# Two modulated norms of a transformer pair by units of two k-tiles through four PSUM banks, evacuated by VectorE alone

## What is computed

```python
def rms_norm_2(x, g):
    y = x32 * lax.rsqrt(jnp.mean(x32 * x32, axis=-1, keepdims=True) + EPS)
    return (y * g).astype(x.dtype)

def modulate(h, shift, scale):
    return h * (1.0 + scale[:, None, :]) + shift[:, None, :]
```

## Time and profile before

| | us |
|---|---|
| median of 3 runs (2705.98 to 2708.37) | 2708.1 |
| profiled execution, its time | 2709.32 |
| its span | 2707.5 |
| TensorE busy | 2627.9 (97%) |
| VectorE busy | 1789.3 (66%) |
| ScalarE busy | 1229.5 (45%) |
| DMA: moved, rate over the span | 581 MB, 215 GB/s |
| granted TensorE clock, mean | 0.988 |

### The profile page before, as it was taken

One profiled execution on the slowest core, in us unless ns is written; L12 is line 12 of the kernel. 1 busy time (PEld: TensorE's weight loads), 2 busy tenths in 40 slices (PEclk: granted clock), 3 DMA queues, 4 the chain that ended last, 5 costly groups with the idle time before them and its releaser, 6 DMA issues.

```text
span 2707.5 us, 35204 instructions
## 1 busy us (share of the span) xinstructions
PE 2627.9 (97%) x12256; PEld 2191.1 (81%) x12256; DVE 1789.3 (66%) x2084; ACT 1229.5 (45%) x1468; POOL 16.0 (1%) x23
## 2 busy tenths in 40 slices
PE   7999999999999999999999899998799999999998
PEld 6888887888878888888888788887678888888886
DVE  5766656557677777777776667875665565555565
ACT  5444456454454444444444544455444443444343
POOL 0000000000000000000000000000000000000000
PEclk9999999999999999999999999999899999999999
DMA  7865555566887777777777577774547666766664
GB/s 269 267 206 167 167 158 184 168 215 195 263 276 250 251 249 249 251 250 249 250 250 243 168 218 216 212 221 132 194 156 223 207 213 200 223 213 207 212 213 133
DMA packets 305304, 581.36 MB, mean 215 GB/s; under 512 B 17728, under 2 KB 28112, under 8 KB 304672
## 3 DMA queue, kind: packets, MB, share of 16 engines
q1 hardware_dynamic: 303664, 573.60, 67.3%
q0 software_dynamic: 1520, 6.11, 0.8%
HBM read 577.53 MB, written 2.11 MB: 214 GB/s over the span
## 4 chain that ended last, share of the span: by engine, by line
PE 85%; DVE 6%; DMA 3%; ACT 3%; issue 2%; SPq 0%; DVEq 0%; ACTq 0%
PE acc L1124 79%; PE W L1124 4%; DVE wlo L1577 2%; DMA raw<-in_w_in 1%; ACT whi L538 1%; PE W L1184 1%; DVE adaacc L1599 1%; DMA raw<-in_w_ffn_in 1%; DMA raw<-in_w_out 1%; ACT arena L565 0%; ACT arena L760 0%; DVE arena L1887 0%; PE W L1296 0%; DVE arena L2185 0%; PE acc L1427 0%
## 5 line engine op out<-in xcount | busy, mean ns | idle before, releaser
L1577 DVE TENSOR_TENSOR wlo<-raw,whi 128x1024 fp32r<-128x1024 f32 x888 | 1080.8, 1224 | 765.2 <-ACT whi L538 762.0
L538 ACT ACTIVATE whi<-raw 128x1024 fp32r<-128x1024 f32 x888 | 934.7, 1059 | 1175.6 <-PE acc L1124 938.4
L1124 PE MATMUL acc<-whi,hH 128*128 128x512 f32 x2528 | 694.0, 396 | 25.7 <-ACT whi L538 19.0
L1124 PE MATMUL acc<-whi,hL 128*128 128x512 f32 x2528 | 679.7, 391 | 0.0
L1124 PE MATMUL acc<-wlo,hH 128*128 128x512 f32 x2528 | 678.4, 390 | 0.0
L1124 PEld LDWEIGHTS acc<-whi,hH 128*128 128x128 f32 x2528 | 470.5, 189 | 119.8 <-issue 27.8
L1124 PEld LDWEIGHTS acc<-whi,hL 128*128 128x128 f32 x2528 | 476.9, 189 | 101.4
L1124 PEld LDWEIGHTS acc<-wlo,hH 128*128 128x128 f32 x2528 | 476.1, 188 | 100.4
L1124 PE MATMUL acc<-whi,yH 128*128 128x512 f32 x992 | 271.0, 395 | 4.8 <-issue 4.8
L1599 DVE SCALAR_TENSOR_TENSOR adaacc<-raw,cs,adaacc 128x512 f32<-128x512 f32 x360 | 269.8, 749 | 8.6 <-DMA raw<-in_w_ada 1.7
L1124 PE MATMUL acc<-wlo,yH 128*128 128x512 f32 x992 | 266.3, 390 | 0.0
(11 more groups left out here) (190 smaller groups left out, 981.4 us busy)
## 6 DMA issues: line engine op xcount, KB each, us to landing
raw<-in_w_in SPq DMA_DIRECT2D x264, 512.0 KB, 4.4
raw<-in_w_ada SPq DMA_DIRECT2D x192, 512.0 KB, 4.7
raw<-in_w_ffn_in SPq DMA_DIRECT2D x176, 512.0 KB, 4.6
raw<-in_w_up SPq DMA_DIRECT2D x128, 512.0 KB, 4.6
raw<-in_w_down SPq DMA_DIRECT2D x128, 512.0 KB, 4.5
raw<-in_w_ffn_out SPq DMA_DIRECT2D x88, 512.0 KB, 4.9
raw<-in_w_out SPq DMA_DIRECT2D x32, 512.0 KB, 5.3
raw<-in_w_o SPq DMA_DIRECT2D x32, 512.0 KB, 4.5
```

Of the source, the lines that this page charges most:

```text
L538: act.activation(whi[:, v], raw[:, s], ACT.Copy).then_inc(S("w_hi"), 1)
L1124: return pe.matmul(o, l, r, start=start, stop=stop, skip_group_check=True)
L1577: dve.tensor_tensor(wlo[:, v], raw[:, s], whi[:, v].bitcast(F32), ALU.subtract)\
```

## The change

- **Units.** The norm goes by eight units of two k-tiles, as the weights do. `scale`, the transposes (4 each), the evacuation, `hH` and `hL` are all by unit, and each weight unit of the first group waits for its own `hL`.
- **Ring.** A unit's transposes go to one of four PSUM banks (`ring`): two of `W`, two of one half of `acc`. TensorE transposes units 0 to 3 ahead of weight unit 0, and unit `u + 4` as a hook behind weight unit `u`, once VectorE has evacuated unit `u` (`h_mod`).
- **Evacuation.** VectorE evacuates both tiles of a unit. ScalarE only copies to `hH`.
- **Column sums.** At the first norm `wlo` of unit 3 moves from ahead of the last column sum to behind unit 0 of the norm (`between`), and `whi` of unit 3 moves behind the root. The sum waits for the same product as before. At the second norm only `wlo` of unit 0 stays ahead; those of 1 (with the adaLN step), 2 and 3 go behind units 0, 1 and 2 of the norm, the small modulation goes behind the last row product, and `whi` of units 1 to 3 go behind the root and behind `hH` of unit 1.
- **Table.** `root_table` moves ahead of all squares at the first norm, and ahead of the last three `w_o` groups at the second.
- GpSimd's two clears wait for the new counts of `h_lo`. `w` loads, products and their counts stay.

```diff
+        def ring(u, g):
+            b = W[:, u % 2] if u % 4 < 2 else acc[:, g % 2, u % 2 * GCOL:(u % 2 + 1) * GCOL]
+            return b.rearrange("p (k t) -> p k t", t=T)
+        def base(index):
+            return 4 if index == 2 else 12
...
-            def modulated(index, a, shift, odd):
-                for c in range(4):
-                    ps = odd if c % 2 else turned
-                    act.wait_ge(S("h_turn"), 4 * (index - 1) + c + 1)
-                    for m in (2, 3):
-                        j = 4 * c + m
-                        ins = act.activation(h32[:, j], ps[:, m * T:(m + 1) * T], ACT.Identity,
-                                             scale=modA[:, a, j:j + 1], bias=mod[:, shift + j:shift + j + 1])
-                    ins.then_inc(S("h_part"), 1)
-                    act.wait_ge(S("h_part"), 4 * (index - 2) + c + 1)
-                    norm_hi(index, c, h32)
+            def modulated(index, between={}):
+                for u in range(8):
+                    q = slice(KU * u, KU * (u + 1))
+                    act.wait_ge(S("h_mod"), 8 * (index - 2) + u + 1)
+                    act.activation(hH[:, q], h32[:, q], ACT.Copy).then_inc(S("h_hi"), 1)
+                    if u in between:
+                        between[u]()
...
-            for c, ahead in enumerate((0, 2, 2, 0)):
+            root_table()
+            for c, ahead in enumerate((0, 2, 1, 0)):
...
                     hi()
-                if c == 3:
-                    root_table()
...
             root(2)
-            modulated(2, 0, 0, acc[:, (PHASES["cmp_kv"][1] + 1) % 2])
+            hi()
+            modulated(2)
...
                 return run
+            root_table()
...
             hi()
-            hi()
             square_o(2)()
-            hi()
-            hi()
-            root_table()
...
             root(4)
-            modulated(3, 2, 48, acc[:, (PHASES["ffn2"][1] + 1) % 2])
+            hi()
+            hi()
+            modulated(3, {1: hi})
...
                 def run(u):
-                    if u % 2 == 0:
-                        pe.wait_ge(S("h_lo"), 4 * (index - 1) + u // 2 + 1)
+                    if index > 1:
+                        pe.wait_ge(S("h_lo"), base(index) + u + 1)
+                    elif u % 2 == 0:
+                        pe.wait_ge(S("h_lo"), u // 2 + 1)
...
-            def modulated(index, odd):
-                for c in range(4):
-                    pe.wait_ge(S("xn"), 4 * (index - 2) + c + 1)
-                    if c >= 2:
-                        pe.wait_ge(S("h_ready"), 4 * (index - 1) + c - 1)
-                        pe.wait_ge(S("h_part"), 4 * (index - 2) + c - 1)
-                    turn(cols(O, c), odd if c % 2 else turned, "h_turn")
+            def turn_unit(index, u, g):
+                pe.wait_ge(S("xn"), 8 * (index - 2) + u + 1)
+                if u >= 4:
+                    pe.wait_ge(S("h_mod"), 8 * (index - 2) + u - 3)
+                for k in range(KU):
+                    for t in range(TT):
+                        ins = pe.transpose(ring(u, g)[:, k, t * P:(t + 1) * P],
+                                           O[:, t, (KU * u + k) * P:(KU * u + k + 1) * P], ident)
+                ins.then_inc(S("h_turn"), 1)
+            def modulated(index, g):
+                for u in range(4):
+                    turn_unit(index, u, g)
+                def later(u):
+                    return lambda: turn_unit(index, u, g)
+                return {u: later(u + 4) for u in range(4)}
...
             down1(11, (("ff_sum", 39), ("ff_sum", 40)), last=True)
-            modulated(2, acc[:, (PHASES["cmp_kv"][1] + 1) % 2])
+            turns2 = modulated(2, PHASES["cmp_kv"][1] + 1)
...
             gg = PHASES["cmp_kv"][1]
-            group(8, hH, hL, (("ff_sum", 43),), ready=h_ready(2))
+            group(8, hH, hL, (("ff_sum", 43),), ready=h_ready(2), hooks=turns2)
...
                 group(4, hH, hL, frees[i:i + 1], ready=om_ready, hooks=hooks)
-            modulated(3, acc[:, (PHASES["ffn2"][1] + 1) % 2])
+            turns3 = modulated(3, PHASES["ffn2"][1] + 1)
...
                 pl.phase("ffn2" if down else "ffn2_first")
-                turns = {1: lambda: turn_square(n, 0), 4: lambda: turn_square(n, 1)} if down else {}
+                turns = {1: lambda: turn_square(n, 0), 4: lambda: turn_square(n, 1)} if down else turns3
...
-            def modulated(k, index, a, shift, odd):
-                def scale(c):
+            def modulated(k, index, a, shift, g, between={}):
+                def scale(u):
+                    q = slice(KU * P * u, KU * P * (u + 1))
                     for t in range(TT):
-                        ins = dve.tensor_scalar(cols(O, c)[:, t], cols(X, c)[:, t], rs[:, k, t:t + 1], None, ALU.mult)
+                        ins = dve.tensor_scalar(O[:, t, q], X[:, t, q], rs[:, k, t:t + 1], None, ALU.mult)
...
-                def evac(c):
-                    dve.wait_ge(S("h_turn"), 4 * (index - 1) + c + 1)
-                    ps = odd if c % 2 else turned
-                    for m in (0, 1):
-                        j = 4 * c + m
-                        ins = dve.tensor_scalar(h32[:, j], ps[:, m * T:(m + 1) * T], modA[:, a, j:j + 1],
+                def evac(u):
+                    dve.wait_ge(S("h_turn"), base(index) + u + 1)
+                    for m in range(KU):
+                        j = KU * u + m
+                        ins = dve.tensor_scalar(h32[:, j], ring(u, g)[:, m], modA[:, a, j:j + 1],
                                                 mod[:, shift + j:shift + j + 1], ALU.mult, ALU.add)
-                    ins.then_inc(S("h_ready"), 1)
+                    ins.then_inc(S("h_mod"), 1)
+                def low(u):
+                    dve.wait_ge(S("h_hi"), base(index) + u + 1)
+                    q = slice(KU * u, KU * (u + 1))
+                    dve.tensor_tensor(hL[:, q], h32[:, q], hH[:, q].bitcast(F32), ALU.subtract).then_inc(S("h_lo"), 1)
...
                 scale(1)
-                evac(0)
-                scale(2)
-                h_low(index, h32, 0)
-                evac(1)
-                scale(3)
-                h_low(index, h32, 1)
-                evac(2)
-                h_low(index, h32, 2)
-                evac(3)
-                h_low(index, h32, 3)
+                for u in range(8):
+                    evac(u)
+                    if u < 6:
+                        scale(u + 2)
+                    low(u)
+                    if u in between:
+                        between[u]()
...
             add_down(2, 11, pl.v - 4)
-            lo(2)
-            add_down(3, 11, pl.v - 4)
+            lo(1)
+            add_down(3, 11, pl.v - 3)
             dve.wait_ge(S("row_cols"), 1)
-            modulated(2, 2, 0, 0, acc[:, (PHASES["cmp_kv"][1] + 1) % 2])
+            modulated(2, 2, 0, 0, PHASES["cmp_kv"][1] + 1, {0: lo})
...
             pl.phase("ffn2_first")
-            lo(4)
-            modulation(20, 60, 80)
-            then(scaled(2, "pre_ffn", 64, 1.0))
+            lo(1)
...
             by_row(3, ("o_sum", 0), 0)()
+            modulation(20, 60, 80)
+            then(scaled(2, "pre_ffn", 64, 1.0))
...
             dve.wait_ge(S("x_mix"), 4)
-            modulated(4, 3, 2, 48, acc[:, (PHASES["ffn2"][1] + 1) % 2])
+            modulated(4, 3, 2, 48, PHASES["ffn2"][1] + 1, {0: lo, 1: lo, 2: lo})
```

4 lines of the change are left out of this document (2 added, 2 removed).

## The result

The changed kernel takes **2713.3 us** (median of 16 runs, 2708.5 to 2719.05), the kernel before beside it 2707.9 (16 runs, 2703.7 to 2709.5). The ratio is 1.0023, 95% interval 1.0015 to 1.0031, so +6.2 us (4.1 to 8.4). The forecast was 2711.0 in a range of 2706 to 2715.5. A second series on another chip gave 2716.6, ratio 1.0030 (1.0018 to 1.0041). The sign was right; the size was about half.

The account below looks back on a forecast made before the run. TensorE, busy 2627.9 of 2707.5 us, was taken as the bound, leaving about 80 us idle to win. First norm +1.9 and second +1.0 gave +2.9 us, 2711.0 from a median of 2708.1; range 2706 to 2715.5.

Parts of the forecast that it names:

- The sign: Whole kernel: slower, by +2.9 us.
- unit 0: First weight unit after the first norm: starts at 1510.7 and not 1515.22, 4.5 us won.
- unit 4: First unit not prepared ahead: starts 0.3 to 1.6 us later at first norm, -0.5 to +0.7 at second.
- slow rows behind it: Products at low clock after the wait before unit 4: 0 to 2.2 us, taken 0.9, at each norm.
- behind the norms: Rotation wait (1.3 us) and relu and `whi` wait (2.15 us) keep their cause; nothing added.
- The head: Ahead of each norm's scaling: earlier column sum and table load bring scaling 2.45 us earlier at first, 5.7 at second.
- the wait before unit 4: TensorE waits for `whi`, queued on ScalarE behind the eighth `hH` copy: about 3.1 us first norm, 2.7 second.
- The low clock behind the two units 0: Slow products at unit 0 of each norm: 0.9 to 2.2 us.
- the restart of 2.15 us: TensorE after the relu and `whi` wait behind the first up group: four products took 1.17, at 2.4 GHz.
- The rival that the clock stays high: Both waits before unit 4: no slow products behind them, +1.1 us, 2709.2; chance 0.27.
- The rival of the raw buffers: Loads behind the first norm restart 6 us later and the lateness stays: +6.9 us, 2715; chance 0.07.
- VectorE's evacuating alone: VectorE needs 2.1 us per further unit against TensorE's 2.72, so it isn't the bound from unit 0 on.

Follow-up runs that it names:

- heads_only: Kernel before with only the changed order ahead of the norms (table, sums, late `wlo` and `whi`), old chunks kept: 2700.7 us, ratio 0.9966; again 2701.7, 0.9979.
- early4: Changed kernel with `whi` of units 4 and 5 ahead of the last `hH` copies, their `wlo` behind `hL` 5 and 6: 2706.1 us, ratio to before 0.9990.
- first_only: Kernel before with the first norm by units and its changed head, second norm and head as before: 2710.9 us, ratio 1.0003.
- unit0_early: early4 with only three transpose units ahead of unit 0, later `wlo`, and `whi` of unit 6 also early: 2703.5 us, ratio to before 0.9983.
- mix: First norm by units as in early4, second in old chunks with the changed head as in heads_only: 2702.4 us, ratio to before 0.9983.
- mix_cover: mix with unused products filling TensorE's waits at both norms: 2700.7 us, ratio to before 0.9973.
- cover_heads: heads_only with 17, 48 and twice 8 unused products in TensorE's waits of the norms: 2697.6 and 2700.0 us, ratios to before 0.9960 and 0.9972.
- second_only: Kernel before with the second norm by units and its changed head, first norm and head as before: 2710.5 us, ratio 1.0007.
- cover_again: Not defined by name in the text; apparently cover_heads repeated on the same chip as the heads_only repeat: 2700.0 us, ratio to before 0.9972.

## Why the prediction came out as it did

The changed trace runs 0.31 us ahead of the old one at the first norm and 3.10 behind it at the second (1499.24 for 1499.55, 1951.74 for 1948.64); the times below are shifted back by that.

| step | forecast | measured |
|---|---|---|
| first norm: squares end, scaling, first transposes | 1502.2, 1503.04, 1503.7 | 1502.2, 1503.0, 1503.7 |
| unit 0 | 1510.7 | 1510.6 |
| last transposes end | 1524.3 to 1525.6 | 1525.1 |
| unit 4 | 1527.4 to 1528.7, taken +1.0 | 1528.3, +1.2 |
| slow rows behind it | 0 to 2.2, taken 0.9 | 2.8 |
| second norm: first transposes, unit 0 | 1959.6, 1967.7 | 1959.8, 1967.9 |
| unit 4 | 1984.1 to 1985.4, taken +0.1 | 1985.2, +0.5 |
| slow rows behind it | 0 to 2.2, taken 0.9 | 1.5 |
| behind the norms | 0 | +1.6 behind the wait of 2.15, -0.6 elsewhere |
| sum | +2.9 | +7.0 |

**The mechanism was right.** The head gives what was summed (in heads_only the wait ahead of the first transposes shrinks by 2.5 us, 6.88 to 4.39, and by 5.6, 16.99 to 11.38), unit 0 starts where forecast to 0.2 us, and the wait before unit 4 has its cause and length (3.1 and 2.7 forecast, 3.20 and 2.79 measured). early4 removed it by order alone.

**The term that failed is the clock.** Three slow terms were taken as 0.9, 0.9 and 0; they measured 2.8, 1.5 and some 1.6. That is 4.1 us too little, as much as the whole difference between +2.9 and +7.0; the other rows of the table miss by +0.2, +0.4 and -0.6 and cancel. The profiled execution lies 3 us above the changed kernel's median, so a typical execution may have fewer slow rows; against the medians' +5.5 the sum is 2.6 us short. That the time still fell inside the range is owed to the width given for the clock, not to the value taken for it. The low clock behind the two units 0, priced at 0.9 to 2.2, measured 1.5 and 1.6. Two errors are in it. The bound of 2.2 for one restart came from a single one, and four rows and not three were slow after 3.20. And I took the restart of 2.15 us, fast in the trace of before, as fast for good, while it was slow in 7 of the 14 profiles. For a term that can come out either way one trace gives one draw, and the sum should carry the frequent value of each restart and not one row of the old trace. The rival that the clock stays high (0.27) is what the profile of first_only shows at the first norm; of 22 runs of the changed kernel one is below that rival's 2709.2. The Trainium skill, page "TensorE: Matmul & The Clock Gate", section "HAM oscillation — how this bites in real kernels", has only longer gaps than these cost the clock. The measurement decides: rows were slow behind 2.15, 2.79 and 3.20 us (granted clock 0.70 behind the last, 1.00 with it filled). The same page's section "What's actually happening" has the number of slow products at the start of a kernel vary from run to run. Here it varied whether rows behind a wait in mid-kernel were slow at all: 7 of 14 profiles behind the wait of 2.15 us.

**The rival of the raw buffers** was not the result here: the rotation's wait is 1.2 us, as before, and ScalarE waits 17.4 us for these loads where it waited 19.6. Once the wait before unit 4 is gone, the traces show late loads as what comes next (unit0_early, mix), though no run tests that by itself.

**What the units are worth.** Against heads_only, the first norm by units wins 2.1 us at unit 0, and pays four transposes between units (0.45 each), 3.2 of wait and 2.8 of slow rows. At the second it wins 0.9 (19.2 for 20.2 us from the last product to unit 0), since an adaLN step of 1.2 us now stands ahead of the second evacuation. Even without the wait (mix) nothing is left of the win, and with the waits filled (mix_cover against cover_heads) A is 1.8 us longer with units than with chunks. VectorE's evacuating alone was not a limit: between units 1 and 3 TensorE waited for nothing; ahead of unit 0 it waited 0.76 and 2.31 us for VectorE's scaling.

Open: which executions have slow rows behind a wait of 2 to 3 us, and what sets the wait near 2295 us that was 0.68 in one profile of the changed kernel and 2.10 in the other. So why the changed kernel spreads over 10.5 us, second_only over 12.1 and cover_again over 1.7 is not shown in full.

## What to carry to other kernels

When work is moved behind other engines' work to start sooner, look at what stands last in each in-order queue: here the copy for unit 4 stood behind the eighth of eight copies, and its wait cost more than the earlier start gave. Test the parts of a change apart: the head alone was worth 0.2 to 0.3%, hidden by the rest. A wait of 2 to 3 us of TensorE in the middle of its work should be priced with up to 3 us of slow products on top, and if it can't be removed, filling it is worth a try: here it gave 1.7 us.

## What the runs showed of the hardware

- After 3.20 us of idle time (3.21 in the second profile) the products ran at 1.2 GHz for 6.5 us in two profiles (2.8 us lost) and not at all in a third with the same wait; with 2.7 us of idle work in it, not at all (granted clock 1.00 for 0.70).
- Work that nobody uses is a gain: 17, 48 and twice 8 products in TensorE's waits, some 18 us of it, made the kernel 1.7 us faster on one chip and raised the mean granted clock from 0.989 to 0.994.
- Eight transposes of 128x128 took 1.97 us at the low clock and 1.09 at the high one; so a short wait costs at every restart on the path, in small operations too.
- The table load of 1.28 us, moved into other work, cost nothing that shows: in heads_only the waits ahead of the first transposes shrank by 2.5 and 5.6 us, as summed with the load at nothing.
